# A transformer step with product-key experts: the gates of tokens 0 to 127 written into a device-memory table by indirect adding transfers instead of one-hot products, with edits at both ends and at the passage between the expert stages

## The reference

```python
def peer_chunk(h, w_q, sub_keys, u_tab, v_tab):
    ...
    s1, i1 = lax.top_k(s[:, :, 0], PEER_TOPK)
    s2, i2 = lax.top_k(s[:, :, 1], PEER_TOPK)
    ...
    top_s, top_i = lax.top_k(cand, PEER_TOPK)
    e = jnp.take_along_axis(cidx, top_i, axis=-1)
    g = jax.nn.softmax(top_s, axis=-1)
    a = jax.nn.gelu(jnp.einsum('cpkd,cd->cpk', u_tab[e], h)).astype(jnp.float32)
    return jnp.einsum('cpk,cpkd->cd', (g * a).astype(v_tab.dtype), v_tab[e])
...
h = layer_norm(ALPHA * x + m, ln1_g, ln1_b)
y = layer_norm(ALPHA * h + peer(h), ln2_g, ln2_b)
```

## Time and profile before

| | us |
|---|---|
| runs shown (3) | 1087.26, 1088.27, 1092.47; median 1088.27 |
| profiled execution, its own time | 1088.31 |
| its span (first to last record) | 1086.6 |
| PE busy | 1051.5 (97%) |
| VectorE (DVE) busy | 856.9 (79%) |
| ScalarE (ACT) busy | 554.6 (51%) |
| GpSimd (POOL) busy | 129.5 (12%) |

### The profile page before, as it was taken

The page is one execution under the profiler, slowest core; times in us unless marked ns, Lnnn a source line. Parts: engine busy times, 40 slices in busy tenths (PEclk is TensorE's granted clock), DMA queues, the critical chain, the costliest instruction groups (busy, mean ns, idle before and its releaser), DMA issues.

```text
span 1086.6 us, 23507 instructions
## 1 busy us (share of the span) xinstructions
PE 1051.5 (97%) x7240; PEld 947.6 (87%) x7240; DVE 856.9 (79%) x1948; ACT 554.6 (51%) x1051; POOL 129.5 (12%) x151
## 2 busy tenths in 40 slices
PE   6999998899999999999999999999999999999996
PEld 6997746799999999999999999998788888888875
DVE  4334387788988989878559999978888888888887
ACT  5425475454544444334555555545555555555543
POOL 0244400000001000544000000000111111110100
PEclk9999999999999999999999999999999999999998
DMA  7655933323568776999863444458888888888862
GB/s 256 258 209 179 348 119 117 135 100 136 173 215 288 250 227 231 390 382 386 297 215 123 144 145 145 144 175 297 303 294 283 294 284 292 286 294 284 295 237 92
DMA packets 96248, 253.19 MB, mean 233 GB/s; under 512 B 11424, under 2 KB 44224, under 8 KB 95408
## 3 DMA queue, kind: packets, MB, share of 16 engines
q1 hardware_dynamic: 81840, 196.84, 52.6%
q0 software_dynamic: 14368, 55.87, 14.7%
HBM read 232.60 MB, written 22.12 MB: 234 GB/s over the span
## 4 chain that ended last, share of the span: by engine, by line
PE 88%; DMA 5%; DVE 4%; ACT 2%; issue 1%; SPq 0%; DVEq 0%; ACTq 0%
PE ps L555 14%; PE ps L556 14%; PE ps L557 13%; PE ps L1029 10%; PE ps L1031 10%; PE ps L1030 10%; PE ps L1002 5%; DMA activations<-u_out 4%; PE ps L639 1%; PE ps L924 1%; DVE w_lo L1406 1%; DMA a_in<-activations 1%; PE ps L1016 1%; PE ps L937 0%; ACT w_hi L1077 0%
## 5 line engine op out<-in xcount | busy, mean ns | idle before, releaser
L1406 DVE TENSOR_TENSOR w_lo<-ring,w_hi 128x512 fp32r<-128x512 f32 (+1 forms) x462 | 394.3, 857 | 134.8 <-ACT w_hi L1077 121.4
L1077 ACT CAST w_hi<-ring 128x512 fp32r<-128x512 f32 (+1 forms) x460 | 345.8, 752 | 94.4 <-PE ps L1031 62.0
L555 PE MATMUL ps<-h_hi,w_hi 128*128 128x256 f32 (+1 forms) x1128 | 330.5, 293 | 3.3 <-DVE w_lo L1406 3.3
L556 PE MATMUL ps<-h_lo,w_hi 128*128 128x256 f32 (+1 forms) x1128 | 321.0, 285 | 0.0
L557 PE MATMUL ps<-h_hi,w_lo 128*128 128x256 f32 (+1 forms) x1128 | 319.3, 283 | 0.0
L555 PEld LDWEIGHTS ps<-h_hi,w_hi 128*128 128x128 f32 x1128 | 214.9, 191 | 7.5 <-issue 4.6
L556 PEld LDWEIGHTS ps<-h_lo,w_hi 128*128 128x128 f32 x1128 | 214.2, 190 | 0.0
L557 PEld LDWEIGHTS ps<-h_hi,w_lo 128*128 128x128 f32 x1128 | 211.8, 188 | 0.0
L1029 PE MATMUL ps<-w_hi,y_hi 128*128 128x512 f32 x512 | 199.6, 390 | 1.0 <-DVE y_lo L1886 1.0
L1031 PE MATMUL ps<-w_lo,y_hi 128*128 128x512 f32 x512 | 199.2, 389 | 0.0
L1030 PE MATMUL ps<-w_hi,y_lo 128*128 128x512 f32 x512 | 199.2, 389 | 0.0
(11 more groups left out here) (355 smaller groups left out, 1233.6 us busy)
## 6 DMA issues: line engine op xcount, KB each, us to landing
ring<-in_uT_dram SPq DMA_DIRECT2D x128, 512.0 KB, 3.6
ring<-in_v_dram SPq DMA_DIRECT2D x128, 512.0 KB, 4.7
activations<-u_out SPq DMA_DIRECT2D x128, 128.0 KB, 3.3
a_in<-activations SPq DMA_DIRECT2D x128, 128.0 KB, 4.1
ring<-in_w_in_dram SPq DMA_DIRECT2D x22, 512.0 KB, 4.3
ring<-in_w_q_dram SPq DMA_DIRECT2D x16, 512.0 KB, 3.2
ks<-in_cache_sb_dram POOLq DMA_DIRECT2D x16, 256.0 KB, 3.2
vs<-in_cache_sb_dram POOLq DMA_DIRECT2D x16, 256.0 KB, 5.7
```

What stands on the lines that cost most here:

```text
L555: mm(out, hi, hi_, start=start, stop=False)
L556: mm(out, hi, lo_, start=False, stop=False)
L1077: nc.scalar.copy(w_hi[slot][:, x], ring[:, ring_slot, x]).then_inc(part_hi, 2 if half is None else 1)
L1406: V.tensor_tensor(w_lo[slot][:, x], ring[:, ring_slot, x], w_hi[slot][:, x].bitcast(F32), ALU.subtract).then_inc(part_lo[ring_slot], 2 if ...
```

## The change

1. **Gates of tokens 0 to 127.** A table of 128 x 128 x 128 floats (8.4 MB) in device memory, `g_dram`, is cleared by SP with eight transfers of 1 MB from a zeroed 128 x 128 tile (512-byte runs). DVE now routes tokens 0 to 127 first, works out the position of each of their 128 slots in the table (`spread_at`) and the gate (`spread_out`); POOL adds them with 128 indirect transfers of 128 single floats each (one slot of all 128 tokens per transfer), and waits after every 16 (one head) until they have landed. 40 of them stand ahead of the gathers of `u` rows, 28 between the gathers, 60 behind. When all are in and PE has done 112 tiles of `u`, POOL loads the table (eight transfers of 1 MB) to `gates[:, 0]`. One-hot products remain for tokens 128 to 255: 16 tiles instead of 32, and `U_ALONE` is 112.
2. **Passage.** The first four activation tiles are loaded early, to a place of their own (`a_first`). `h` is added with an fp32r identity of 1 instead of a float32 one of `ALPHA`; in exchange the gates are divided by `ALPHA` and the layer norm's epsilon by its square.
3. **End.** The last four tiles of `v` have places of their own for weights and activations; PE adds them to `tt = 0` first, all four, and then to `tt = 1`, so that the norm of `tt = 0` can run beside the latter.
4. **Start.** The first weight tile is split in halves, with the first tile of x between, and ACT's table is loaded before it waits for data.

```diff
-        gates = at("gates", [128, NE, DT], at_a)
+        gates = at("gates", [128, 2, NE, 128], at_a)
...
-        scaled_id = at("scaled_id", [128, 128], at_x + 8 * T - 128)
+        whole_id = at("whole_id", [128, 128], at_x + 8 * T - 128, F32R)
...
-        U_ALONE = NE - DT // 8
+        U_ALONE = NE - GN // 8
...
             for n in (0, 1, 3):
                 load(AT_OUT + n, w_out[n])
+            sp.wait_ge(cmp_clear, 1)
+            for q in range(8):
+                sp.dma_start(g_rows[:, 16 * q:16 * (q + 1), :],
+                             spread_out[:, :].unsqueeze(1).to_broadcast([128, 16, 128])).then_inc(cleared, 16)
             sp.wait_ge(ss_pv, 2)
             for n in (2, 4, 5, 6, 7):
                 load(AT_OUT + n, w_out[n])
...
+            for r in range(2):
+                sp.wait_ge(spill[r], 16 * 2)
+            for r in range(4):
+                sp.dma_start(a_first[:, r, :], a_dram[r]).then_inc(a_full[r], 16)
...
-                if n == NE + 5:
-                    for r in range(2):
-                        sp.wait_ge(spill[r], 16 * 2)
-                    sp.wait_ge(g_mm, 2 + DT // 2)
-                    for r in range(4):
-                        sp.dma_start(a_in[:, r, :], a_dram[r]).then_inc(a_full[r], 16)
...
+            def gates_out(first, last):
+                for m in range(first, last):
+                    if m and m % TOPK == 0:
+                        pool.wait_ge(spread_in, 16 * m)
+                    nc.gpsimd.indirect_dma_start(
+                        g_dram, bass.IndirectOffsetOnAxis(ap=spread_at[:, m:m + 1], axis=0), spread_out[:, m:m + 1],
+                        None, compute_op=ALU.add).then_inc(spread_in, 16)
+
+            ahead = 8 * TOPK - 88
+            pool.wait_ge(cleared, 16 * 8)
+            pool.wait_ge(spread_ready, 1)
+            gates_out(0, ahead)
             pool.wait_ge(ix_ready, 1)
             for k in range(SLOTS):
                 if k >= 4:
                     pool.wait_ge(u_dot, k - 3)
                 nc.gpsimd.indirect_dma_start(urow[:, k % 4, :], None, u_rows, at_slot(k)).then_inc(ug_in[k % 4], 16)
+                if k >= 4:
+                    gates_out(ahead + k - 4, ahead + k - 3)
+            gates_out(ahead + SLOTS - 4, 8 * TOPK)
+            pool.wait_ge(spread_in, 16 * 8 * TOPK)
+            pool.wait_ge(w_mm, 2 * (AT_U + U_ALONE))
+            for q in range(8):
+                pool.dma_start(gates[:, 0, 16 * q:16 * (q + 1), :], g_rows[:, 16 * q:16 * (q + 1), :]).then_inc(gates_in, 16)
...
-            with pe.Fori(0, DT // 32) as i:
+            with pe.Fori(0, GN // 32) as i:
...
-                        ins = mm(ps[:, bank, c * 128:(c + 1) * 128], part[:, bank % 2 * 4 + c, tok].bitcast(F32),
-                                 scaled_id[:, :], start=part is h_hi and c == 0, stop=False, skip_group_check=True)
+                        ins = mm(ps[:, bank, c * 128:(c + 1) * 128], part[:, bank % 2 * 4 + c, tok],
+                                 whole_id[:, :], start=part is h_hi and c == 0, stop=False, skip_group_check=True)
...
+            for q in range(LAST):
+                n = NE - LAST + q
+                pe.wait_ge(y_l, n + 1)
+                for half in range(2):
+                    lows = halves(0, AT_V + n)
+                    pe.wait_ge(lows[0], lows[1 + half])
+                    ins = down_part(0, half, last(q), N_W + q, q == LAST - 1)
+            ins.then_inc(d_mm, 1)
+            for half in range(2):
+                for q in range(LAST):
+                    ins = down_part(1, half, last(q), N_W + q, q == LAST - 1)
+                ins.then_inc(d_mm, 1)
...
-            high_of(0)
+            nc.scalar.preload_act_table_set(log_and_exp)
+
+            high(0, 16, 0, 0)
             for c in range(KD):
                 act.wait_ge(x_in[c // 2], 16)
                 nc.scalar.copy(x_hi[:, c, :], xTs[:, c, :]).then_inc(x_h, 1)
+                if c == 0:
+                    high(0, 16, 0, 1)
...
-            with act.Fori(0, U_ALONE // 4 - 3) as i:
+            with act.Fori(0, 5) as i:
                 for r in range(4):
                     gelu_then_high(i, r, 4)
+            act.wait_ge(rt_exp_in, 1)
+            A(pick[:, 0, 2, :], pick[:, 0, 2, :], ACT.Exp).then_inc(rt_exp, 1)
...
+            route(0, 8, pick[:, 0, 2, :])
+            link(V.scalar_tensor_tensor(posf[:, :], pick[:, 0, 0, :], 128.0, pick[:, 0, 1, :], ALU.mult, ALU.add))
+            link(V.tensor_tensor_reduce(rowo[:, :], k("ident"), k("iota"), 1.0, 0.0, ALU.mult, ALU.add, token[:, :]))
+            link(V.scalar_tensor_tensor(posf[:, :], posf[:, :], 128.0, token[:, :].to_broadcast([128, 128]),
+                                        ALU.mult, ALU.add))
+            link(V.tensor_copy(spread_at[:, :], posf[:, :]))
+            dve.wait_ge(cleared, 16 * 8)
+            normalise(pick[:, 0, 2, :].rearrange("p (h k) -> p h k", k=TOPK), 8, 1, spread_out[:, :].rearrange("p (h k) -> p h k", k=TOPK)).then_inc(spread_ready, 1)
             route(2, 2, sgate[:, :])
...
-            for tt in range(2):
-                route(tt, 8, pick[:, tt, 2, :])
+            route(1, 8, pick[:, 1, 2, :])
             dve.wait_ge(hr_sb, 1)
             for j in range(SLOTS):
                 dve.wait_ge(ug_in[j % 4], 16 * (j // 4 + 1))
...
-            with dve.Fori(0, DT // 32) as i:
+            with dve.Fori(0, GN // 32) as i:
...
+            dve.wait_ge(gates_in, 16 * 8)
```

More of the change, by code:

```diff
@@ L1052, in _ @@
                 mm(ps[0:32, 4 + half, :], k("fold"), sacc[:, x], start=True, stop=False)
-                ins = mm(ps[0:32, 4 + half, :], scaled_id[0:32, 0:32], hrow[0:32, x], start=False, stop=True)
+                ins = mm(ps[0:32, 4 + half, :], ident[0:32, 0:32], hrow[0:32, x], start=False, stop=True)
             ins.then_inc(f_mm, 1)
-            for r in range(8):
+            for r in range(4):
                 n = NE - 8 + r
-                experts_down(r % 4, halves(0, AT_V + n), n + 1, False, r == 7)
+                experts_down(r, halves(0, AT_V + n), n + 1)
+            last = lambda q: (y_hi_last[:, q, :], y_lo_last[:, q, :])
+            for q in range(LAST):
[10 more added lines that the diff above has]
+                ins.then_inc(d_mm, 1)
         @block.scalar
@@ L1320, in _ @@
             nc.scalar.copy(hrow[:, :].rearrange("p (a b) -> p a b", b=512), ps[:, 4:6, :]).then_inc(hr_sb, 1)
-            with act.Fori(0, U_ALONE // 4 - 3) as i:
+            with act.Fori(0, 5) as i:
+                for r in range(4):
+                    gelu_then_high(i, r, 4)
+            act.wait_ge(rt_exp_in, 1)
+            A(pick[:, 0, 2, :], pick[:, 0, 2, :], ACT.Exp).then_inc(rt_exp, 1)
+            for r in range(4):
+                gelu_then_high(5, r, 4)
+            with act.Fori(6, U_ALONE // 4 - 3) as i:
                 for r in range(4):
@@ L1326, in _ @@
             A(sgate[:, :], sgate[:, :], ACT.Exp).then_inc(rt_exp, 1)
-            for tt in range(2):
-                A(pick[:, tt, 2, :], pick[:, tt, 2, :], ACT.Exp).then_inc(rt_exp, 1)
+            A(pick[:, 1, 2, :], pick[:, 1, 2, :], ACT.Exp).then_inc(rt_exp, 1)
             for r in range(8):
@@ L1416, in low_next @@
                 lows[0] = n + 1
-            low_next()
+            low(1, 0, 0, 0)
             for c in range(KD):
@@ L1971, in _ @@
                 z = ztok[:, tt, :]
-                dve.wait_ge(d_mm, tt + 1)
-                both_halves(1 + tt, every, 2 * tt)
+                for half in range(2):
+                    dve.wait_ge(d_mm, 1 if tt == 0 else 2 + half)
+                    ins = V.bn_stats(stats[:, 1 + tt, half, :], ps[:, 2 * tt + half, :])
+                link(ins)
                 variance(1 + tt, every)
```

167 lines of the change are left out of this document (101 added, 66 removed).

## The result

| | before | after |
|---|---|---|
| median of the runs, us | 1087.8 (4 runs, 1086.2 to 1092.5) | 1128.9 (4 runs, 1126.5 to 1131.3) |
| profiled execution, span | 1086.6 | 1129.7 |

The changed kernel is slower: the ratio is 1.0371, with a 95% interval of 1.0338 to 1.0404. The forecast was 1078 with a range to 1110, so sign and range were both missed. Where single executions of one kernel lie more than 1.5% apart, its ratio is taken from the faster ones alone.

The account below looks back on a forecast made before the run. PE, busy for 97% of the span, was taken as the bound, with DVE also full in the one-hot stage. From 1088.3 us, -29 + 22 + 4 - 3 - 2 - 2 = -10 gave 1078 us, range 1051 to 1110.

Parts of the forecast that it names:

- adding transfers and what waits behind: POOL's 128 transfers delay gathers and dot products, which end at about 544 instead of 514 us: +22 us.
- load of the table: 8.4 MB load beside the one-hot tiles takes 44 us, there by 690, before the stage ends at 706: nothing.
- clearing: Clearing the table in SP's queue takes 43 us at 42 ns a run, delaying `w_out` loads: +4 us, between 0 and 35.
- passage: The 64 matmuls with `scaled_id`, 7.15 us, get up to half as long as fp32r: -3 us, between -3.5 and 0.
- start: Table load of 1.28 us goes off the path and halves let DVE begin earlier: -2 of 2.5 us kept.
- end: Less norm work stands behind PE's last matmul, -4, but PE waits about 2 for y: -2 us, between -4 and +1.
- The step that failed: On POOL, an adding transfer costs what a gather does, 0.89 + 0.30 us, plus a wait for DVE's running operation.
- Rival C: POOL's list and the gathers' queue: an adding transfer is dearer than a gather, 1.9 us, kernel slower at 1114; chance 0.20.
- A: POOL keeps up, paying 1.24 us a transfer in DVE's pauses; only the gains remain, 1056 us; chance 0.28.
- A second step: In the dot-product stretch, PE lives on tiles DVE has done ahead, some 9 us; the transfers' term is +22 us.
- rival E: The table is late: if the last head lands after 665, DVE stands before the first weighting, us for us; chance 0.05.
- Rival D: Clearing takes its upper price, 75 us, to 220; `w_out` loads come 33 us late, 1107 us; chance 0.07.

Follow-up runs that it names:

- e_ahead: Changed kernel with only the 40 adding transfers ahead of the gathers, the other 88 left out: 1093.8 us, ratio 1.0052 to the kernel before.
- e_pahead: Changed kernel with only the 40 transfers ahead of the gathers, as plain writes, 88 left out: 1088.0 us (1075.3 to 1103.8), too far apart for a ratio.
- e_pbetween: Changed kernel with only the 28 transfers between the gathers, as plain writes, 100 left out: 1083.4 us, ratio 0.9943 to the kernel before.
- e_between: Changed kernel with only the 28 adding transfers between the gathers, the other 100 left out: 1091.3 us, ratio 1.0032 to the kernel before.
- e_none: Changed kernel without its 128 adding transfers, clearing and table load kept: 1063.2 us, ratio 0.9777 to the kernel before.
- b_all: Kernel before with only the start, passage and end edits, no table and no adding transfers: 1083.2 us, ratio 0.9948 to the kernel before.
- e_order0: Changed kernel with no adding transfers ahead of the gathers, 28 between and 100 behind, nothing left out: 1158.0 us, ratio 1.0644 to the kernel before.

## Why the prediction was wrong

Against the profiled span, +43.1 us instead of -10, term by term:

| term | predicted | measured | from |
|---|---|---|---|
| half of the one-hot work | -29.0 | -29.0 | +61.1 at tile 91 to +32.1 at 120 |
| adding transfers and what waits behind | +22 | +59.7 | +1.4 at tile 53 to +61.1 at 91 |
| load of the table | 0 | +15.8 | +32.1 to +47.9 |
| clearing | +4 | +2, but not shown to be the clearing's | below |
| passage | -3 | -3.5 | +47.8 to +44.3 |
| start | -2 | -1.3 | SP's loads of `w_out` at 138.5, not 139.8 |
| end | -2 | -1.2 | +44.3 to +43.1 |
| put down to the early Exp on ACT, not shown | not seen | +0.7 | tile 1 to tile 53 |

**The step that failed** is "how long one takes no row shows; the nearest is the gather": the price of an adding transfer, taken as 0.89 + 0.30 us as for a gather and half a wait for DVE. It is 1.55 + 0.30 before any wait. Rival C had this price and this place in POOL's list (1.9 us, forty ended at 453, dot products at 580, PE loses 58); measured were 1.85 us, 457, 577 and 59.7. Its other place, the queue of the gathers, was not borne out (e_ahead). Its time of 1114 was still 15 short, which is the table. It was given 0.20, and A, in which POOL keeps up, 0.28. Nothing in the trace of before spoke for "as a gather" more than for "dearer": the reason for rival C, that each float must be read, added and written, was in the text and was not priced into the middle. The plain writes show that this very step is the difference: without the addition the instruction takes a gather's 0.97 us, the forty ahead end at 436 (e_pahead; 438 forecast), and the cycle of the dot products is 3.2 us (e_pbetween; 3.2 forecast).

**A second step** made it worse by some 5 us: that PE would pay 8 of the 30 us by which the dot products end later (544 instead of 514) from the tiles that DVE had done ahead, "some 9 us". In e_ahead, e_between and e_pbetween dot products that ended 29, 28 and 14 us later than in e_none made the kernel 31, 28 and 16 us longer (the last by the spans). PE had already starved in that stretch before the change (81.8 of 85 us); it started five tiles there only when their low part was done. PE's waits between 470 and 515, before:

```profile
PE ps L555 <- DVE w_lo L1406: 3.2, 5, 1.0
```

So its tiles ahead were used up there in any case, and a delay could not be paid from them a second time. In the changed kernel the dot products ended 62.7 us later than before (577.2), and PE stood 59.4 behind at tile 80: of the 8 us counted on, 3 were there. Together: 22, 33 for dot products that end at 577 rather than 544, and 5 are 60.

**The table** was held to be covered if it came by 690, and rival E priced only its lateness. The load was issued at 716.7 instead of 642 (E on top of C), but e_none shows that it costs 7 us even when it is issued at 615.6, in a stage with 0.56 of DMA's time free: over the whole stage the bytes fit, but loaded at once they filled DMA (0.95 of its time from 615 to 640), and the stores of activations that ACT waits for came late. Issued at 716.7 it cost twice that. A part of it is PE's clock, which was granted at 0.66 from 735 to 740 and at 0.82 from 750 to 760, behind waits of 2.5 and 9.0 us. The row of the changed kernel, ACT between 720 and 750:

```profile
ACT u_out L1352 <- DMA activations<-u_out: 20.7, 3, 13.1
```

Rival D was wrong, and the bound under the clearing was the better one. SP's eight transfers, and DMA in 139 to 170 in 40 slices:

```profile
139.81 26.98 SPq L434 DMA_DIRECT2D gates<-spread_out  x8
```

```profile
DMA  0973677999999999999999999999999999999999
GB/s 0 458 250 122 233 241 278 354 356 366 373 357 285 291 349 348 348 347 348 348 347 323 334 340 348 348 349 348 347 346 347 348 347 349 349 348 344 348 348 340
```

348 GB/s over 16 engines is 24 ns for a run of 512 bytes, not 42. (The Trainium skill, DMA: Bandwidth & Descriptors, section "Specifications", puts 512 B at line rate; by that rule the clearing was to cost nothing, and the trace agrees with it.) The low part of tile 2 of `w_out` came at 184.0 instead of 182.2; b_all, which has the same start and no clearing, has it at 181.8. But the 2 us between them are there at 155 already, before the loads behind the clearing matter: PE's clock was granted at 0.66 from 145 to 150. Of the fifteen profiled kernels with the clearing, five have a clock of 0.66 to 0.68 there and begin tile 1 at +0.4 to +2.6; of the ten with 1.00 nine begin it at -2.3 to -0.6 (e_order0 at +0.5), all nine earlier than b_all at +0.4. So no run shows a cost of the clearing itself.

With a gather's price and the other terms as measured (27 for the wait, 7 for an early table), the sum would be -29 + 27 + 7 + 2 - 3.5 - 1.3 - 1.2 + 0.7, about +2: an estimate, but it says that the price alone turned a change without gain into a loss of 41 us. (A slip without effect: by the prediction's own 2.83 us a tile, tile 112 would be done at 636, not 632.)

**What held.** The first transfer began at 370.2 (371 forecast); one-hot tiles, passage (64 matmuls in 3.6 us instead of the 7.15 of the earlier trace rows, 0.056 each, just under the lower bound given) and end behaved as worked out. At the end PE did wait for the y of the last tiles (once 1.07 us, up to 1114.53). PE's last matmul came 46.8 us late where its first of the stage was 44.3 late, so the waits took 2.5 of the 3.7 us that the shorter tail gave; against the earlier trace rows DVE has one statistic less behind PE (1123.24 is its last). The start's gain, 8.65 to 6.33 us for PE's first matmul, was 1.3 at 138 us.

POOL's waits for DVE were read rightly in kind: with DVE idle the transfers take 1.55, beside its two-input operations up to 2.89, and beside searches or a reduction of 2.28 us (at 385.5 and 409.9) again 1.55. (The Trainium skill, GPSIMD Engine Reference, section "Key points", names such operations as the ones that contend; the trace agrees. It does not bear on the larger part, the 0.58 us of the addition, which is there with DVE idle.)

## What to carry to other kernels

Where the deciding term is the price of an operation that no row shows, multiply it by its count before choosing: at 128 times, the 0.58 us that an addition takes more than a gather are 74 us, so the likeliest case must be the one whose extra work is known to be there, not the nearest row. An engine with a share of 12% is no free engine for work that stands ahead of something others wait for; add up its list and hold it against the time from the first input to the last deadline (here 300 us of work in the 271 between 371 and 642) before asking in which order it is done. And slack that the profile of before already shows as starved is not a reserve.

## What was not expected of the hardware

- An adding transfer is paid per instruction on POOL, hardly per element: 1.55 us for 128 floats, 1.40 for 64; a plain write of 128 floats 0.97. In DMA it is the other way: the packets under 512 bytes were 30,112 with the additions, 11,680 without any (144 for each of 128 transfers), 21,921 with 64 floats (80 each) and 15,776 as plain writes (32 each), so an addition has a packet for each float, and 16 more.
- 8.4 MB loaded beside a stage with 0.56 of DMA's time free cost 7 us, at once or an eighth at a time, by way of 128 KB stores that landed late while DMA was full (0.95 of its time from 615 to 640 in e_none).
- Plain writes of single floats left DMA nearly idle at times with loads and stores outstanding (one wait of 21 us, with DMA at 0.02 of its time from 410 to 420), and scattered the times of e_pahead from 1075 to 1104 us; sixty alone at another place did nothing. Unexplained.
